# Two transformer blocks on one Trainium2 core: another order of the opening, of the softmax's steps on VectorE, and one up-projection over 256 tokens instead of two over 128

## What is computed

```python
mx = jnp.split((silu_c @ ada_w[i] + ada_b[i])[:, None, :], N_MOD, axis=-1)
mc = jnp.split(silu_cc @ ada_w[i] + ada_b[i], N_MOD, axis=-1)
h_x = modulate(rms_norm(x, g[0]), mx[0], mx[1])
h_c = modulate(rms_norm(ctx, g[0]), mc[0], mc[1])
...   # layer 0: attention with a sink column, over x (banded) and context; layer 1: RG-LRU
p = jax.nn.softmax(jnp.concatenate([s_loc, s_ctx, sink_col], axis=-1), axis=-1)
x = x + mx[2] * rms_norm(y_x, g[1])
x = x + mx[5] * rms_norm(sqrelu_mlp(modulate(rms_norm(x, g[2]), mx[3], mx[4]), mlp_w1[i], mlp_w2[i]), g[3])
```

## Time and profile before

| | us |
|---|---|
| median of 3 runs | 1770.12 |
| lowest and highest of them | 1767.89, 1770.85 |
| the profiled execution's own time | 1767.38 |
| its span (first to last instruction) | 1765.6 |
| PE busy | 1617.0 (92%) |
| DVE busy | 1107.0 (63%) |
| ACT busy | 862.2 (49%) |

### The profile page before, as it was taken

The page is one execution under the profiler, slowest core; times in us unless marked ns, Lnnn a source line. Parts: engine busy times, 40 slices in busy tenths (PEclk is TensorE's granted clock), DMA queues, the critical chain, the costliest instruction groups (busy, mean ns, idle before and its releaser), DMA issues.

```text
span 1765.6 us, 24431 instructions
## 1 busy us (share of the span) xinstructions
PE 1617.0 (92%) x8850; PEld 1330.8 (75%) x8850; DVE 1107.0 (63%) x1817; ACT 862.2 (49%) x1404; POOL 13.1 (1%) x36
## 2 busy tenths in 40 slices
PE   4999989899999999898779999798888799999999
PEld 3754548888888888777569999696566798978888
DVE  2345663744444456689955666687466578687795
ACT  3234545723333327587744444544333466556573
POOL 2000000000000000000000000000000000000000
PEclk9989999899999999999866999899898799999999
DMA  8377742323333322332423666352221289878792
GB/s 317 102 304 257 254 188 72 116 79 101 97 95 95 95 85 71 96 95 84 128 75 96 186 185 188 108 169 93 84 72 36 71 287 345 296 257 328 275 340 113
DMA packets 195802, 279.72 MB, mean 158 GB/s; under 512 B 12434, under 2 KB 111220, under 8 KB 190588
## 3 DMA queue, kind: packets, MB, share of 16 engines
q1 hardware_dynamic: 194308, 274.21, 46.7%
q0 software_dynamic: 1152, 4.19, 0.6%
q10 hardware_dynamic: 248, 0.09, 0.0%
HBM read 277.40 MB, written 1.05 MB: 158 GB/s over the span
## 4 chain that ended last, share of the span: by engine, by line
PE 73%; DVE 15%; ACT 7%; issue 3%; DMA 1%; SPq 0%; DVEq 0%; ACTq 0%; POOL 0%; POOLq 0%
PE bank L433 63%; DVE weights_lo L406 3%; PE bank L701 2%; ACT weights_hi L394 1%; PE bank L1306 1%; PE bank L1290 1%; DVE work L2636 1%; PE bank L1274 1%; DVE work L2673 1%; DVE work L2683 1%; DMA x_and_ctx<-in_ctx_dram 1%; DVE x_and_ctx L2636 1%; DVE x_and_ctx L553 1%; DVE work L2515 1%; ACT work L543 1%
## 5 line engine op out<-in xcount | busy, mean ns | idle before, releaser
L406 DVE TENSOR_TENSOR weights_lo<-stage,weights_hi 128x1024 fp32r<-128x1024 f32 x332 | 394.3, 1220 | 81.7 <-ACT weights_hi L394 78.1
L394 ACT ACTIVATE weights_hi<-stage 128x1024 fp32r<-128x1024 f32 x332 | 337.8, 1055 | 150.5 <-PE bank L433 102.2
L433 PE MATMUL bank<-act_hi,weights_hi 128*128 128x256 f32 (+2 forms) x1072 | 346.6, 323 | 18.2 <-DVE weights_lo L406 9.6
L433 PE MATMUL bank<-act_lo,weights_hi 128*128 128x256 f32 (+2 forms) x1072 | 344.2, 321 | 0.0
L433 PE MATMUL bank<-act_hi,weights_lo 128*128 128x256 f32 (+2 forms) x1072 | 344.0, 321 | 0.0
L433 PEld LDWEIGHTS bank<-act_hi,weights_hi 128*128 128x128 f32 x1072 | 216.7, 202 | 34.0 <-DVE weights_lo L406 11.3
L433 PEld LDWEIGHTS bank<-act_lo,weights_hi 128*128 128x128 f32 x1072 | 217.0, 202 | 11.2
L433 PEld LDWEIGHTS bank<-act_hi,weights_lo 128*128 128x128 f32 x1072 | 216.7, 202 | 11.1
L433 PE MATMUL bank<-weights_hi,ff_hi 128*128 128x512 f32 x560 | 220.9, 395 | 1.9 <-DVE ff_lo L2850 1.9
L433 PE MATMUL bank<-weights_hi,act_hi 128*128 128x512 f32 (+1 forms) x488 | 197.5, 405 | 25.0 <-DVE act_lo L2697 16.2
L433 PE MATMUL bank<-weights_hi,ff_lo 128*128 128x512 f32 x560 | 220.2, 393 | 0.0
(11 more groups left out here) (395 smaller groups left out, 2057.0 us busy)
## 6 DMA issues: line engine op xcount, KB each, us to landing
stage<-in_mlp_w_dram SPq DMA_DIRECT2D x128, 512.0 KB, 4.0
stage<-in_w_dram SPq DMA_DIRECT2D x96, 512.0 KB, 6.0
ada_rows_in<-in_ada_w_dram SPq DMA_DIRECT2D x40, 1024.0 KB, 5.5
x_and_ctx<-in_w_dram SPq DMA_DIRECT2D x48, 512.0 KB, 6.0
work<-in_w_dram SPq DMA_DIRECT2D x48, 512.0 KB, 6.5
stage<-in_w_in_dram SPq DMA_DIRECT2D x32, 512.0 KB, 4.4
stage<-in_lru_w_in_dram SPq DMA_DIRECT2D x20, 512.0 KB, 4.4
stage<-in_attn_w_qkv_dram SPq DMA_DIRECT2D x12, 512.0 KB, 4.7
```

Source lines behind the costliest of these rows:

```text
L394: act.eng.activation(whi[u % NRING][:], landing(act, u)[:], ACT.Copy).then_inc(sem("hi_ready"), 1)
L406: dve.eng.tensor_tensor(wlo[u % NRING][:], landing(dve, u)[:], whi[u % NRING][:].bitcast(F32), ALU.subtract).then_inc(sem("lo_ready"), 1)
L433: m = pe.eng.matmul(ps, l, r, start=start and j == 0, stop=stop and j == 2, skip_group_check=True)
```

## The change

SP issues x and context first, before the parameter rows. `norm_act` and `norm_dve` work by pairs of tiles, x and then context, each with its own root. PE takes all eight pieces of the first half of the modulation before it turns the first tokens. The second half's loads are issued later: POOL's and SP's once piece 6 of the first half has landed, SP's behind two units of weights instead of one. The second half's columns are brought into place in the middle of the second unit of `qkv(0)` instead of after it. ACT and DVE take the first half's sums ahead of the first weight split. In the attention DVE scales half h-1 before it takes the maximum of half h. In layer 1 both tiles are turned first, and each of the four units is then multiplied once with 256 columns.

```diff
-        def norm_act(act, tag, tiles, xn, shift, src_ready=None):
-            for n, tt in enumerate(tiles):
-                if src_ready:
-                    act.eng.wait_ge(*src_ready(n))
-                act.eng.activation(xn[:, n, :], XC[:, tt, :], ACT.Square,
-                                   accum_out=ss[:, n:n + 1]).then_inc(*act.mark("norm_ss"))
-            act.eng.wait_ge(*norm_at(tag, "ms", 1))
-            act.eng.activation(rstd[:, 0:len(tiles)], ss[:, 0:len(tiles)], ACT.Sqrt).then_inc(*act.mark("norm_sd"))
...
-        def norm_dve(dve, tag, tiles, xn):
...
-            for j, tt in enumerate(tiles):
-                dve.eng.tensor_scalar(xn[:, j, :], XC[:, tt, :], ss[:, 4 + j:5 + j], None, ALU.mult).then_inc(*dve.mark("norm_xn"))
+        def norm_act(act, tag, pairs, xn, src_ready):
+
+            for g, tiles in enumerate(pairs):
+                act.eng.wait_ge(*src_ready(g))
+                for tt in tiles:
+                    act.eng.activation(xn[:, tt, :], XC[:, tt, :], ACT.Square,
+                                       accum_out=ss[:, tt:tt + 1]).then_inc(*act.mark("norm_ss"))
+                at = slice(tiles[0], tiles[-1] + 1)
+                act.eng.wait_ge(*norm_at(tag, "ms", g + 1))
+                act.eng.activation(rstd[:, at], ss[:, at], ACT.Sqrt).then_inc(*act.mark("norm_sd"))
...
+        def norm_dve(dve, tag, pairs, xn):
+
+            for g, tiles in enumerate(pairs):
+                at, root = slice(tiles[0], tiles[-1] + 1), slice(4 + tiles[0], 5 + tiles[-1])
+                dve.eng.wait_ge(*norm_at(tag, "ss", tiles[-1] + 1))
...
+                dve.eng.reciprocal(ss[:, root], rstd[:, at]).then_inc(*dve.mark())
+                dve.eng.wait_ge(*dve.own())
+                for tt in tiles:
+                    dve.eng.tensor_scalar(xn[:, tt, :], XC[:, tt, :], ss[:, 4 + tt:5 + tt], None,
+                                          ALU.mult).then_inc(*dve.mark("norm_xn"))
...
-        FF = {"m0_first": 8, "m0_last": 8, "m1_first": 8, "m1_last": 4}
+        FF = {"m0_first": 8, "m0_last": 8, "m1_first": 4, "m1_last": 4}
...
-                            if n == 0 and 2 * tt % ntt == 0:
+                            if n == 0 and 2 * tt % ntt == 0 and FF[group] >= 4 * half + 4:
...
-                    if n == 0 and kq == 1:
+                    if n == 0 and kq == 2:
+                        sp.eng.wait_ge(sem(first_full(0, 6)), 16)
                         first_ada_load(sp.eng, 1, 4, 8)
...
             t.wait_ge(sem("pick"), 1)
-            first_ada_pe(pe, 0, 1, 0, 2)
-            first_turns(0, 3)
             t.wait_ge(sem("rows"), 16 * len(ROWS))
             ps = pe.take("params", 2)
             for n in range(2):
                 m = t.transpose(ps[:, n * P:(n + 1) * P], prow[:, n, :], ident[:])
             m.then_inc(*pe.fill("params"))
-            first_ada_pe(pe, 0, 1, 2, 8)
+            first_ada_pe(pe, 0, 1, 0, 8)
+            first_turns(0, 2)
             first_cols_pe(pe, 0, 1)
+            first_turns(2, 3)
...
+                        if n == 0 and kq == 1 and tt == 1:
+                            first_cols_pe(pe, 1, 7)
                     unit_end(pe, m, ("qkv", n, 3) if kq == 3 else None)
...
                     if n == 0 and kq == 1:
-                        first_cols_pe(pe, 1, 7)
                         first_turns(5, 8)
...
-            TOK = [slice(0, P), slice(P, TX)]
             turn_pe(pe, "n1b", 0, lambda tt: xn_a[:, tt, :])
-            first_hidden("m1f", "n1b", TOK, lambda: turn_pe(pe, "n1b", 1, lambda tt: xn_a[:, tt, :]))
+            turn_pe(pe, "n1b", 1, lambda tt: xn_a[:, tt, :])
+            u0, hviews = pe.unit, []
+            for m in range(4):
+                hviews.append(unit_begin(pe, (KT, P)))
+                hidden_pe(pe, "m1f", 0, m, hviews, XTOK,
+                          (lambda k: turned_at("n1b", "lo", 1, max(k, 1))) if m == 0 else None, True, u0 + m)
...
-            norm_act(act, "n0", FOUR, xn0, True, lambda n: (sem(("x_in", "ctx_in")[n // 2]), 16))
+            norm_act(act, "n0", PAIRS, xn0, lambda g: (sem(("x_in", "ctx_in")[g]), 16))
...
+            first_ada_act(act, 0)
             split_hi(act, 1)
-            first_ada_act(act, 0)
...
             turn_act(act, "n1b", 0, True)
-            split_hi(act, 2)
-            for m in (0, 1):
-                hidden_act(act, "m1_first", m, "m1f", 0, m, slice(0, P))
             turn_act(act, "n1b", 1, True)
-            for m in (2, 3):
-                hidden_act(act, "m1_first", m, "m1f", 0, m, slice(0, P))
-            split_hi(act, 2)
+            split_hi(act, 3)
             for m in range(4):
-                hidden_act(act, "m1_first", 4 + m, "m1f", 1, m, slice(P, TX))
-                split_hi(act, 1)
+                hidden_act(act, "m1_first", m, "m1f", 0, m, slice(0, TX))
+                split_hi(act, 2 if m == 3 else 1)
             split_hi(act, 2)
...
-            norm_dve(dve, "n0", FOUR, xn0)
+            norm_dve(dve, "n0", PAIRS, xn0)
             v.wait_ge(*dve.freed("params"))
+            first_ada_dve(dve, 0)
             split_lo(dve, 1)
-            first_ada_dve(dve, 0)
...
             for h in range(34):
+                if 1 <= h < 33:
+                    g = h - 1
+                    nk = P * len(key_tiles(HALVES[g][3]))
+                    at = 2 * (g % 2)
+                    cols2 = slice(at, at + 2)
+                    v.wait_ge(sem("exps"), g + 1)
+                    v.tensor_tensor(sm[:, 3, cols2], sm[:, 1, cols2], sm[:, 2, cols2], ALU.add).then_inc(*dve.mark())
+                    v.wait_ge(*dve.own())
+                    v.reciprocal(sm[:, 3, cols2], sm[:, 3, cols2]).then_inc(*dve.mark())
+                    v.wait_ge(*dve.own())
+                    for i in range(2):
+                        v.tensor_scalar(prob[g % 3][:, i, 0:nk], prob[g % 3][:, i, 0:nk], sm[:, 3, at + i:at + i + 1],
+                                        None, ALU.mult).then_inc(*dve.mark("p_norm"))
                 if h < 32:
...
                 if h - 1 in ADA_TURN:
                     ada_dve(dve, ADA_TURN[h - 1])
-                if 1 <= h < 33:
-                    g = h - 1
...
-                                        None, ALU.mult).then_inc(*dve.mark("p_norm"))
...
             turn_dve(dve, "n1b", 0, True)
-            split_lo(dve, 2)
-            for m in (0, 1):
-                hidden_dve(dve, "m1_first", m, m, slice(0, P))
             turn_dve(dve, "n1b", 1, True)
-            for m in (2, 3):
-                hidden_dve(dve, "m1_first", m, m, slice(0, P))
-            split_lo(dve, 2)
+            split_lo(dve, 3)
             for m in range(4):
-                hidden_dve(dve, "m1_first", 4 + m, m, slice(P, TX))
-                split_lo(dve, 1)
+                hidden_dve(dve, "m1_first", m, m, slice(0, TX))
+                split_lo(dve, 2 if m == 3 else 1)
...
-            g.wait_ge(sem(first_full(0, 3)), 16)
+            g.wait_ge(sem(first_full(0, 6)), 16)
             first_ada_load(g, 1, 0, 4)
...
             sp = Lane(e, "sp", plan)
+            e.dma_start(XC[:, 0:2, :], x_v).then_inc(sem("x_in"), 16)
+            e.dma_start(XC[:, 2:4, :], ctx_v).then_inc(sem("ctx_in"), 16)
             e.wait_ge(sem("prow_zero"), 1)
             for tile, r, src in ROWS:
                 e.dma_start(prow[r:r + src.shape[0], tile, :], src).then_inc(sem("rows"), 16)
-            e.dma_start(XC[:, 0:2, :], x_v).then_inc(sem("x_in"), 16)
-            e.dma_start(XC[:, 2:4, :], ctx_v).then_inc(sem("ctx_in"), 16)
```

21 lines of the change are left out of this document (4 added, 17 removed).

## The result

The changed kernel takes 1724.97 us (median of 4 runs, 1721.45 to 1727.04) against 1769.01 for the one before on the same chips (4 runs, 1764.89 to 1770.85): ratio 0.9752, 95% interval 0.9728 to 0.9777, 44 us less. Forecast were 1731.5, 38.5 less, with the range 1721 to 1744. The main case came true; the size is 5.5 short.

A forecast was written before the change was run, and what follows sets the result against it. The prediction saw a row of stages in which PE is the limit or waits for DVE and ACT; opening 7.7, attention 5.2 and layer 1 25 sum to 38, and 0.5 for a clock drop gives 1731.5 us, range 1721 to 1744.

The forecast's parts named there:

- The main case: Whole kernel: opening, attention and layer 1 all give about what is said, 1724 to 1738; chance 0.70.
- 8 turns at the low clock 1.9: Opening, after the first half's last piece and products: eight token turns take 1.9 us at the low clock.
- 24 matmuls 7.30: Opening, first projection unit: its 24 matmuls take 7.30 us, the same work as before.
- I take 1.6, the middle: Opening: the transfer stream begins 1.6 us earlier, between nothing and 3.2, so at 3.9.
- the count of 12 pieces of 1.38: Opening: the first half's last piece is number 12, landing at 3.9 + 12 x 1.38 = 20.5 us.
- Again behind the weight splits, 1.0: Attention, step 28: exponentials no longer hidden behind the weight splits that stop DVE, a cost of 1.0 us.
- 1.0 for a rest of low clock: Layer 1, first group: 1.0 us charged for matmuls still at low clock.
- 1.2 of idle between the tiles: Layer 1: 1.2 us of idle between the two tiles, counted as part of the gain.
- The rival of a clock that stays low: Layer 1: the clock stays at 0.50, giving 18 us in place of 25, total 1738.5; chance 0.10.
- The attention's ring: Attention: DVE and ACT wait 0.2 us more a half, 6.4 in all, so the gain is gone, 1737; chance 0.10.
- its rival: Opening bound by bytes: stream begins as before, second half's pieces stop PE, 3 us in place of 7.7, 1736; chance 0.08.
- fall to 1.2 GHz: Attention's PE work doubles at the low clock, up to 1800 us, slower than before; chance 0.02.

The follow-up runs named there:

- n1: The changed kernel with layer 1's first group multiplied with 128 columns twice instead of once with 256; 1752.41 us, ratio 0.9907.
- o1: The changed kernel with SP's six parameter rows issued ahead of x and context again; 1732.40 us.
- n3_narrow_lifted: The changed kernel with layer 1's first group at 128 columns twice, plus 14 unused matmuls of 512 columns in PE's wait ahead of it; 1730.01 us, ratio 0.9786.

## Why the prediction was right, and where it was short

**Opening: 7.7 forecast, 9.7 measured.** Right in kind: transfers bound it up to the last piece, which came at 20.25 (20.5), the norm left the chain (its scaling ended at 18.7, not before 17, but PE asks for it at 20.86), and the second half's last piece came at 34.65 (34.3). The first matmul stood at 25.54, not 26.8. The step that was off is "8 turns at the low clock 1.9": they took 1.09. The same for "24 matmuls 7.30": 5.86 from 25.54 to the turns at 31.40, since the clock didn't fall. Together 2.2 more. Where the fall came (n1), the opening still took 51.47, 8.4 less than before. Against that the 64 small matmuls waited 0.15 for a transfer and took 3.95 instead of 3.59, and the columns in the middle gave 1.2 (1.4). "I take 1.6, the middle" for the earlier stream was too little: undone, it costs 2.9 of transfers (o1). That the landing came right all the same is luck: from a beginning at 5.5 - 2.9 = 2.6 the count of 12 pieces of 1.38 gives 19.2, and they took 1.1 longer, so that two errors cancel.

**Attention: 5.2 forecast, 8.7 measured.** The chain of the changed kernel, 130 to 178 us (start us, us, what), over a plain pair, answers to the earlier trace rows:

```profile
144.16 1.90 PE bank L1314 x32
146.06 1.02 PE bank L1298 x8
147.09 1.00 PE bank L707 x8
...
148.30 1.06 PE bank L1282 x4
149.36 1.02 PE bank L1298 x8
150.38 1.00 PE bank L707 x8
...
151.59 1.06 PE bank L1282 x4
152.65 1.90 PE bank L1314 x32
```

DVE's timeline in the same stretch:

```profile
151.18 0.16 DVE L2501 TENSOR_TENSOR softmax_cols<-softmax_cols 128x2 f32<-128x2 f32 x1 [1.41 <-ACT softmax_cols L2018]
...
151.58 0.88 DVE L2506 TENSOR_SCALAR work<-work,softmax_cols 128x512 f32<-128x512 f32 x2
152.38 1.28 DVE L2515 TENSOR_REDUCE softmax_cols<-bank 128x1 f32<-128x512 f32 x2
...
155.86 0.88 DVE L2506 TENSOR_SCALAR work<-work,softmax_cols 128x512 f32<-128x512 f32 x2
```

From values to values it is 8.49, forecast 8.6. DVE's ring is 155.86 - 151.58 = 4.28 a half, forecast 4.25, with DVE waiting 1.41 for ACT as foreseen; PE's own work, 8.5, is as long, and the chain shows PE alone. Term by term, from the starts of the values: the six plain pairs of 512 keys give 2.9 (2.0 forecast for five), the two with columns 4.9 (3.0; 3.2 and 1.7, and 1.5 of the 3.2 is the clock's fall near 153), the pairs of 256 keys 1.7 (2.7), the pipeline's filling costs 0.9 (1.5), and step 28 nothing (1.0). "Again behind the weight splits, 1.0" was a cost that didn't come. The clock is a gain that I booked with 0.5 and that came out at 2.1; nothing in the prediction derives that part, and whether the order brings it is open, so that the size of this stage's gain owes something to it. At equal clock the order gives 6.5 against the 5.2 forecast.

**Layer 1: 25 forecast, 26.8 measured.** Table of stretches of the changed kernel, the 96 matmuls and the 48 behind them, to be read against the earlier trace rows:

```profile
896.70:910.42 13.72, 13.72 (x96) 13.72 (x97) 10.01 (x18) 11.75 (x23) 0.00 (x0) 0.82 0.49 130
910.42:921.33 10.91, 10.91 (x50) 9.02 (x49) 7.45 (x9) 4.95 (x6) 0.00 (x0) 1.00 0.82 254
```

The first matmul at 896.70 is, moved by the 16.1 us that the stretch lies earlier, 912.8 (forecast 912.9); the first unit ends at 901.8, moved 917.9 (917.7); the other 72 take 8.6 (8.7); the 48 take 10.91 (10.9). The term that was off is "1.0 for a rest of low clock": the clock rose at 901.6, with the end of the first unit. Another 0.7 was rounded away: 24.1 + 1.6 is 25.7, not 25. "1.2 of idle between the tiles" is a wrong reading that the sum doesn't use: 930.76 - 907.16 - 20.71 is 2.9. The rival of a clock that stays low is dead here, and n1_narrow shows what it would have cost with 128 columns.

The reason that I gave for the gain was half as many weight loads at the same time each, and the clock for the rest. The runs give a number for each: 192 narrow ones take 41.0 at 0.50 (192 x 0.2133), the same 192 take 21.45 at 1.00, and the 96 wide ones, a slow first unit among them, 13.7. Counted in this order, the clock first, it has 19.5 of these 27.3 and the width 7.8. But the shares hang on the order. Wide ones at 0.50 would take 96 x 0.213 = 20.4 (an estimate from the first unit, 24 in 5.10), so counted the other way the width has 20.6 and the clock 6.7: either alone brings some 20 of the 27.3, since each about halves the time of a stretch that is slow for both reasons. To the 27.3 come the 48 matmuls behind (12.62, now 10.91) and the pause between the tiles (2.9), less the start that is 5.6 later. "The same time each" holds too: a weight load takes 192 ns in n3_narrow_lifted and in the changed kernel at 1.00. Whether it is the load that a narrow matmul waits for, no run separates.

The Trainium skill, "TensorE: Matmul & The Clock Gate", section "Loop structure matters more than you think", was weighed in the prediction: matmuls back to back keep the array at full clock. These runs hold a half of it: n3_narrow_lifted's 192 kept a clock that was full. n1_narrow's 192, as dense, never got there.

**Rivals.** The attention's ring was not worse than the old one; the opening's chain follows transfers up to 34, as its rival had it, but they cost PE only 0.15 us there, and the stream did begin earlier; the attention didn't fall to 1.2 GHz but for 7.2 us.
